# A three-block transformer kernel on one core: the opening's loads cut by partitions, and three late products and roots placed elsewhere

## The chip, the cores and the metric

The kernel runs on one core of a Trainium2 chip. The metric is the device time of the whole program in microseconds (us). The core has five engines that run side by side and meet only at semaphores: TensorE (PE in the rows, its weight load PEld), VectorE (DVE), ScalarE (ACT), GpSimd (POOL) and SyncE (SP). Transfers are issued here from the instruction streams of SP and ACT. Each of the two has a queue of its own (q1 for SP, q10 for ACT in the profile), and both queues are served by the core's 16 DMA engines.

## The reference, cut to what matters

Three transformer blocks work on one sequence of 512 tokens with 1024 channels, each a mixer and a SwiGLU feed-forward part with root-mean-square norms between them.

```python
def reference(x, ...):
    x = first_block(...)      # norm, x @ w_in, pooling + dilated attention, @ w_out, norm, swiglu
    return second_block(...)  # retention + swiglu, then stick-breaking attention + swiglu

def rms_norm(x, g):
    return x * lax.rsqrt(jnp.mean(x * x, axis=-1, keepdims=True) + EPS) * g

def stick_breaking(h, w_in, q_gain, k_gain, w_o):
    q, k, v = jnp.split(h @ w_in, 3, axis=-1)
    q = rms_norm_2(heads(q), q_gain)      # per head of 64
    k = rms_norm_2(heads(k), k_gain)
    ...
```

## The kernel before

**Layout.** Activations stand channels first: the input X is 8 chunks of 128 channels x 512 tokens, 256 KB each. A weight matrix is streamed as units, each giving 128 output channels: 8 chunks of 128x128 (512 KB), or 11 in the down projections.

**Three products for one.** To keep float32 accuracy at the faster matmul type, every operand is split in a high and a low part. ScalarE rounds a landed unit RAW to WH; GpSimd (VectorE in a few places) makes WL = RAW - WH. HH and HL are the high and low part of the input, MH and ML of the feed-forward's hidden values. A unit costs 24 matmuls in a bank B of PSUM: WH x HH and WH x HL for each chunk (`high_part`), then WL x HH for each chunk (`low_part`). The semaphores are `s_hi` and `s_lo` (a unit's WH, WL are ready), `s_hi_used` (WH may be overwritten), `s_unit` (the unit is complete), `s_h_hi` and `s_h` (HH, HL of a chunk are ready).

**The norm is applied late.** HH and HL are the unnormed input times its gain. Squares are added up in ACC, a matmul with the matrix MEAN (or MEANR) gives the mean over channels, ScalarE takes the root of it, and the result RB multiplies the outputs. So a mean can stand anywhere in TensorE's order between the sum being ready and the first use of the root.

**The order** of each engine is written by hand; there is no scheduler. Each engine runs its own list and waits at semaphores.

**The opening.** The first unit (`first_unit`) needs X and unit 0 of the weights, cut in halves of four chunks. SP issues the gains, X1, X2, the second half of unit 0, X4, X6, the first half of unit 1, then unit 2, the constants and so on. ACT issues X0, the first half of unit 0, X3, X5, X7 and the second half of unit 1, and then begins its own work: HH of chunks 0 and 1, WH of the first half of unit 0, HH 2 and 3, WH of the second half, HH 4 to 7, WH of unit 1, and the eight squares SQ4. VectorE makes HL of each chunk and both halves of WL0, then adds the squares. TensorE runs three warm-up products of zeros and then the first unit, chunk by chunk. GpSimd starts WL of unit 1 once all of HL is ready and WL of units 2 to 5 once all squares are added:

```python
pool.wait_ge(s_h, DC)
split_lo(Unit(1), chunks)
pool.wait_ge(s_sq_used, DC)
for n in range(2, 6):
    split_lo(Unit(n), chunks)
```

**Start of the first feed-forward part.** `first_units_after_post` runs three units at once, chunk by chunk, as the updated input arrives. Behind it come units u0+3 and u0+4 in `ffn`, with the mean of the new input (`mean_of_sum`) in the middle of u0+4's high part.

**First stage of the stick-breaking attention.** `stick_stage` projects q, k and v of a pair of heads. The means of squares per head (`head_mean`, 0 for q and 1 for k) stand in TensorE's order around the v unit u+2; ScalarE takes the roots (`rn`), VectorE makes QT and KT from them, and the score products L1184 wait for KT. In the first stage no earlier pair is worked on (`a is None`).

Of the kernel before, what the change touches and what calls it, by code (L numbers as in the profile page):

```python
# [128 lines left out]
def build(nc, ins, out_t):  # L129
    ctx = ExitStack()  # L130
    with ctx:
# [141 lines left out]
        s_second = sem("second_half_weights_landed")  # L273
# [73 lines left out]
        def high_part(pe, u, bank, chunks, xh, xl, k0=0, start=True, halfway=None):  # L347

            wh = WH[u.s]
            pe.wait_ge(s_hi, u.index + 1)  # L350
            for c in range(chunks):
                if halfway is not None and c == chunks // 2:
# [152 lines left out]
        def _(sp):  # L505
# [11 lines left out]
            for count, chunks, large in STRETCHES:  # L517
                stream = ins["w_large" if large else "w_small"].rearrange("u p (c n) -> u p c n", c=chunks)
                start = 0
                if first == 0:  # L520

                    sp.dma_start(GAINS[:], ins["gains"]).then_inc(s_gains, 16)
                    for c in (1, 2):
                        sp.dma_start(X[:, c, :], ins["x_t"][:, c, :]).then_inc(s_x_in[c], 16)
                    sp.dma_start(RAW[0][:, 4:DC, :], stream[0][:, 4:DC, :]).then_inc(s_raw[0], 16)
                    for c in (4, 6):
                        sp.dma_start(X[:, c, :], ins["x_t"][:, c, :]).then_inc(s_x_in[c], 16)
                    sp.dma_start(RAW[1][:, 0:4, :], stream[1][:, 0:4, :]).then_inc(s_raw[1], 16)
                    load_unit(Unit(2), stream[2], chunks)
                    sp.wait_ge(s_x_in[DC - 1], 16)  # L530
# [113 lines left out]
        def _(pe):  # L644
# [62 lines left out]
            def first_units_after_post(u0, which, n, mean):  # L707
# [27 lines left out]
                for bank, _, wl in units:  # L735
                    pe.matmul(bank[:], wl[:, DC - 1, :], HH[:, DC - 1, :], start=False, stop=True).then_inc(s_unit, 1)

            def ffn(f, u0, before, n=None):
# [10 lines left out]
                if before is None:  # L749
# [4 lines left out]
                    high_part(pe, Unit(u0 + 4), B[0][:], DC, HH, HL, halfway=lambda: mean_of_sum(n))  # L754
# [412 lines left out]
            def stick_stage(j, jp, a, ap):  # L1167
# [112 lines left out]
                else:  # L1280
# [43 lines left out]
        def _(act):  # L1324
# [133 lines left out]
            act.dma_start(X[:, 0, :], ins["x_t"][:, 0, :]).then_inc(s_x_in[0], 16)  # L1458
            act.preload_act_table_set(LOG_EXP)
            act.dma_start(RAW[0][:, 0:4, :], small[0][:, 0:4, :]).then_inc(s_first, 16)  # L1460
            for c in (3, 5, 7):
                act.dma_start(X[:, c, :], ins["x_t"][:, c, :]).then_inc(s_x_in[c], 16)
            act.dma_start(RAW[1][:, 4:DC, :], small[1][:, 4:DC, :]).then_inc(s_second, 16)
            act.wait_ge(s_gains, 16)
            for c in range(DC):
                act.wait_ge(s_x_in[c], 16)
                input_hi(c, G_MIX1)
                if c == 1:
                    act.wait_ge(s_first, 16)
                    act.copy(WH[0][:, 0:4, :], RAW[0][:, 0:4, :]).then_inc(s_first_hi, 1)  # L1470
                if c == 3:
                    act.wait_ge(s_raw[0], 16)
                    act.copy(WH[0][:, 4:DC, :], RAW[0][:, 4:DC, :]).then_inc(s_hi, 1)
            act.wait_ge(s_second, 16)
# [194 lines left out]
            def stick_stage(j, jp, a, ap):  # L1669
# [97 lines left out]
                if j is not None:  # L1767
# [52 lines left out]
        def _(dve):  # L1820
# [712 lines left out]
```

## Time and profile before

| | |
|---|---|
| three runs | 1969.74, 1970.10, 1970.29 us; median 1970.1 |
| profiled execution | 1969.64 us, of which span 1967.9 |
| TensorE busy | 1959.1 us of the span |
| VectorE, ScalarE, GpSimd busy | 860.4, 801.4, 769.4 us |
| moved by DMA | 177.37 MB, mean 90 GB/s |
| granted TensorE clock | 1.0 over the whole span |

The time of a run is the span plus what lies around it, 1.7 us in the profiled execution. TensorE's idle time is what is left over between 1967.9 and 1959.1, about 9 us over the whole kernel. The page's slices are 49 us wide, so places of a microsecond are read from the timeline instead.

### The profile page before, as it was taken

The page shows a single profiled execution, that of the slowest core. Times are in us where ns is not written, and L with a number is a line of the kernel's source. Part 1 is how long each engine was busy: PE and PEld are TensorE (multiplying, and loading weights), DVE is VectorE, ACT ScalarE, POOL GpSimd, SP SyncE. Part 2 cuts the span into 40 slices and gives each one's busy share as a digit, 9 for nine tenths or more (in the row PEclk, how much of TensorE's full clock was granted, in tenths as well). Part 3 has the DMA queues.
Part 4 walks back from the last instruction along what each step waited for, and adds up shares of the span by engine and source line. Part 5 has one row for each costly group of instructions (what it writes and reads, how often), then busy time and mean ns, then how long its engine had stood idle before and what let it go on. Part 6 is the DMA issues. An engine that isn't in the chain of part 4 may idle for free.

```text
span 1967.9 us, 25769 instructions
## 1 busy us (share of the span) xinstructions
PE 1959.1 (100%) x8956; PEld 1591.1 (81%) x8956; DVE 860.4 (44%) x1142; ACT 801.4 (41%) x1078; POOL 769.4 (39%) x309
## 2 busy tenths in 40 slices
PE   9999999999999999999999999999999999999999
PEld 6777888888888778787888888887777788888887
DVE  5775643433135335334243434224788753433200
ACT  6665533233243433324332223225888752323211
POOL 3223444444423334243444444433222144444443
PEclk9999999999999999999999999999999999999999
DMA  4212122223223222222232223222111122222332
GB/s 172 73 68 86 65 96 96 96 96 114 92 73 123 70 86 91 69 88 83 85 107 96 96 96 111 90 99 84 54 64 53 54 97 96 96 96 96 110 100 90
DMA packets 48867, 177.37 MB, mean 90 GB/s; under 512 B 5552, under 2 KB 6192, under 8 KB 48816
## 3 DMA queue, kind: packets, MB, share of 16 engines
q1 hardware_dynamic: 46656, 173.08, 26.1%
q10 hardware_dynamic: 2160, 3.61, 0.6%
q8 instruction: 33, 0.54, 0.1%
q14 instruction: 18, 0.15, 0.0%
HBM read 174.57 MB, written 2.10 MB: 90 GB/s over the span
## 4 chain that ended last, share of the span: by engine, by line
PE 96%; DVE 2%; ACT 1%; issue 0%; DMA 0%; POOL 0%; SPq 0%; DVEq 0%; ACTq 0%; POOLq 0%
PE B L354 26%; PE B L355 26%; PE B L363 25%; PE B L1068 2%; PE B L1195 1%; PE B L1026 1%; PE B L1030 1%; PE B L1027 1%; PE B L380 1%; PE B L375 1%; PE B L376 1%; PE B L1184 1%; PE B L1112 1%; PE B L1240 1%; PE B L854 1%; PE B L885 1%
## 5 line engine op out<-in xcount | busy, mean ns | idle before, releaser
L588 POOL TENSOR_TENSOR WL<-RAW,WH 128x1024 fp32r<-128x1024 f32 (+1 forms) x298 | 758.4, 2547 | 1173.1 <-PE B L363 768.9
L354 PE MATMUL B<-HH,WH 128*128 128x512 f32 x1608 | 629.2, 391 | 0.2 <-ACT WH L335 0.2
L355 PE MATMUL B<-HL,WH 128*128 128x512 f32 x1608 | 626.1, 389 | 0.0
L335 ACT CAST WH<-RAW 128x1024 fp32r<-128x1024 f32 (+1 forms) x300 | 329.1, 1098 | 550.9 <-PE B L355 478.7
L363 PE MATMUL B<-HH,WL 128*128 128x512 f32 x1608 | 398.3, 390 | 0.0
L354 PEld LDWEIGHTS B<-HH,WH 128*128 128x128 f32 x1608 | 301.9, 188 | 65.3 <-issue 2.3
L363 PEld LDWEIGHTS B<-HH,WL 128*128 128x128 f32 x1608 | 301.4, 188 | 63.1 <-POOL WL L588 0.4
L355 PEld LDWEIGHTS B<-HL,WH 128*128 128x128 f32 x1608 | 301.9, 188 | 62.4
L1850 DVE TENSOR_TENSOR U<-B,RB 128x512 f32<-128x512 f32 x66 | 45.6, 691 | 294.7 <-PE B L363 294.7
L354 PE MATMUL B<-MH,WH 128*128 128x512 f32 x440 | 171.2, 389 | 0.0
L355 PE MATMUL B<-ML,WH 128*128 128x512 f32 x440 | 171.2, 389 | 0.0
L1853 DVE TENSOR_TENSOR HD<-SG,U 128x512 f32<-128x512 f32 x66 | 148.5, 2251 | 7.4 <-ACT SG L1353 0.7
L1357 ACT CAST MH<-HD 128x512 f32 (+1 forms) x66 | 40.9, 620 | 247.3 <-DVE HD L1853 247.3
L1868 DVE TENSOR_TENSOR X<-X,B 128x512 f32 (+1 forms) x32 | 22.0, 687 | 244.2 <-PE B L363 223.2
L1833 DVE TENSOR_TENSOR ACC<-ACC,SQ 128x512 f32<-128x512 f32 x38 | 74.7, 1965 | 118.9 <-ACT SQ L1331 118.8
L363 PE MATMUL B<-MH,WL 128*128 128x512 f32 x440 | 106.2, 389 | 0.0
L354 PEld LDWEIGHTS B<-MH,WH 128*128 128x128 f32 x440 | 82.6, 188 | 17.1
L363 PEld LDWEIGHTS B<-MH,WL 128*128 128x128 f32 x440 | 82.6, 188 | 17.1
L355 PEld LDWEIGHTS B<-ML,WH 128*128 128x128 f32 x440 | 82.6, 188 | 17.1
L1353 ACT ACTIVATE SG<-G 128x512 f32<-128x512 f32 x66 | 41.8, 633 | 88.9 <-DVE G L1848 88.9
L1856 DVE TENSOR_TENSOR ML<-HD,MH 128x512 f32 (+1 forms) x66 | 49.4, 748 | 58.2 <-ACT MH L1357 58.2
L1848 DVE TENSOR_TENSOR G<-B,RB 128x512 f32<-128x512 f32 x66 | 45.6, 691 | 54.7 <-PE B L363 46.2
(349 smaller groups left out, 2246.9 us busy)
## 6 DMA issues: line engine op xcount, KB each, us to landing
RAW<-in_w_small SPq DMA_DIRECT2D x254, 512.0 KB, 3.2
RAW<-in_w_large SPq DMA_DIRECT2D x48, 704.0 KB, 4.1
out_t<-X SPq DMA_DIRECT2D x8, 256.0 KB, 5.1
X<-in_x_t ACTq DMA_DIRECT2D x4, 256.0 KB, 6.3
X<-in_x_t SPq DMA_DIRECT2D x4, 256.0 KB, 6.4
DECAY<-in_decay ACTq DMA_DIRECT2D x4, 256.0 KB, 2.7
RAW<-in_w_small ACTq DMA_DIRECT2D x2, 256.0 KB, 6.6
RAW<-in_w_small SPq DMA_DIRECT2D x2, 256.0 KB, 7.4
```

The lines of the kernel that those rows point to most:

```text
L335: act.copy(wh, raw).then_inc(s_hi, 1)
L354: pe.matmul(bank, wh[:, c, :], xh[:, k0 + c, :], start=(start and c == 0), stop=False)
L355: mm = pe.matmul(bank, wh[:, c, :], xl[:, k0 + c, :], start=False, stop=False)
L363: mm = pe.matmul(bank, wl[:, c, :], xh[:, k0 + c, :], start=False, stop=(stop and c == chunks - 1))
L588: pool.tensor_tensor(wl, raw, wh.bitcast(F32), ALU.subtract).then_inc(s_lo, 1)
L1353: act.activation(SG[:], G1[:], ACT.Silu).then_inc(s_silu, 1)
L1357: act.copy(MH[:, i, :], HD[:]).then_inc(s_m_hi, 1)
L1833: dve.tensor_tensor(ACC[:], ACC[:], SQ[b][:], ALU.add).then_inc(s_sq_used, 1)
L1848: dve.tensor_tensor(G1[:], gate, RB[:], ALU.mult).then_inc(s_gate, 1)
L1850: dve.tensor_tensor(U1[:], up, RB[:], ALU.mult).then_inc(s_up, 1)
L1853: dve.tensor_tensor(HD[:], SG[:], U1[:], ALU.mult).then_inc(s_hidden, 1)
L1856: dve.tensor_tensor(ML[:, i, :], HD[:], MH[:, i, :].bitcast(F32), ALU.subtract).then_inc(s_m, 1)
```

## The change

Four things are changed.

1. **Opening.** Each X chunk and both halves of unit 0 are loaded by two transfers: partitions 0 to 63 from ACT, partitions 64 to 127 from SP. Both queues have the same order: X0, X1, first half of unit 0, X2, X3, second half, X4 to X7, then unit 1 (its halves of four chunks over all 128 partitions, one on each queue as before). Whoever uses a chunk waits for 32 instead of 16. ACT issues X4 and X5 behind its HH 0, X6 and X7 behind HH 1, and its half of unit 1 behind HH 2.
2. **Three low products** of chunk 6 in `first_units_after_post` stand behind the high products of chunk 7, and the high products of chunk 6 wait for HL 6 at once.
3. **The mean** in unit u0+4 of the first feed-forward part stands behind five chunks instead of four.
4. **First stick-breaking stage:** the k mean stands behind six chunks of the v unit's high part instead of behind all eight, and ScalarE takes its root before it rounds unit u+3, not after.

```diff
-                    for c in (1, 2):
-                        sp.dma_start(X[:, c, :], ins["x_t"][:, c, :]).then_inc(s_x_in[c], 16)
-                    sp.dma_start(RAW[0][:, 4:DC, :], stream[0][:, 4:DC, :]).then_inc(s_raw[0], 16)
-                    for c in (4, 6):
-                        sp.dma_start(X[:, c, :], ins["x_t"][:, c, :]).then_inc(s_x_in[c], 16)
+                    for c in range(2):
+                        sp.dma_start(X[64:P, c, :], ins["x_t"][64:P, c, :]).then_inc(s_x_in[c], 16)
+                    sp.dma_start(RAW[0][64:P, 0:4, :], stream[0][64:P, 0:4, :]).then_inc(s_first, 16)
+                    for c in (2, 3):
+                        sp.dma_start(X[64:P, c, :], ins["x_t"][64:P, c, :]).then_inc(s_x_in[c], 16)
+                    sp.dma_start(RAW[0][64:P, 4:DC, :], stream[0][64:P, 4:DC, :]).then_inc(s_raw[0], 16)
+                    for c in range(4, DC):
+                        sp.dma_start(X[64:P, c, :], ins["x_t"][64:P, c, :]).then_inc(s_x_in[c], 16)
...
+            def load_x(c):
+                act.dma_start(X[0:64, c, :], ins["x_t"][0:64, c, :]).then_inc(s_x_in[c], 16)
...
             for c in range(DC):
-                act.wait_ge(s_x_in[c], 16)
+                act.wait_ge(s_x_in[c], 32)
                 input_hi(c, G_MIX1)
+
+                if c < 2:
+                    load_x(2 * c + 4)
+                    load_x(2 * c + 5)
+                if c == 2:
+                    act.dma_start(RAW[1][:, 4:DC, :], small[1][:, 4:DC, :]).then_inc(s_third, 16)
                 if c == 1:
-                    act.wait_ge(s_first, 16)
+                    act.wait_ge(s_first, 32)
                     act.copy(WH[0][:, 0:4, :], RAW[0][:, 0:4, :]).then_inc(s_first_hi, 1)
...
-                for c in range(DC - 1):
+                for c in range(DC - 2):
                     chunk(c, SECOND if c < BY_HALVES else slice(0, T), lambda: pe.wait_ge(s_h_hi, 8 * which + c + 1),
                           lambda: pe.wait_ge(s_h, 8 * which + c + 1))
+                pe.wait_ge(s_h, 8 * which + DC - 1)
+                for bank, wh, _ in units:
+                    pe.matmul(bank[:], wh[:, DC - 2, :], HH[:, DC - 2, :], start=False, stop=False)
+                    pe.matmul(bank[:], wh[:, DC - 2, :], HL[:, DC - 2, :], start=False, stop=False)
...
-                    high_part(pe, Unit(u0 + 4), B[0][:], DC, HH, HL, halfway=lambda: mean_of_sum(n))
+                    high_part(pe, Unit(u0 + 4), B[0][:], DC, HH, HL, halfway=lambda: mean_of_sum(n), at=5)
...
+                    else:
+                        high_part(pe, u + 2, B[0][:], DC, HH, HL, halfway=lambda: head_mean(1, 1), at=6)
...
+                        rn(1, jj, first)
                         split_hi(act, u + 3, DC)
-                        rn(1, jj, first)
                         split_hi(act, u + 4, DC)
```

**ScalarE at the start of the program**, before (its transfers and its work up to the four last chunks of the input):

```order
L1458 DMA X<-in_x_t 128x512
L1459 ACT_TABLE_LOAD
L1460 DMA RAW<-in_w_small 128x512
L1462 DMA X<-in_x_t 128x512 x3
L1463 DMA RAW<-in_w_small 128x512
L1334 ACTIVATE HH<-X,GAINS 128x512 x2
L1470 CAST WH<-RAW 128x512
L1334 ACTIVATE HH<-X,GAINS 128x512 x2
L1473 CAST WH<-RAW 128x512
L1334 ACTIVATE HH<-X,GAINS 128x512 x4
```

and now, up to HH of chunk 2:

```order
L1473 DMA X<-in_x_t 64x512
L1476 ACT_TABLE_LOAD
L1473 DMA X<-in_x_t 64x512
L1478 DMA RAW<-in_w_small 64x512
L1473 DMA X<-in_x_t 64x512 x2
L1481 DMA RAW<-in_w_small 64x512
L1347 ACTIVATE HH<-X,GAINS 128x512
L1473 DMA X<-in_x_t 64x512 x2
L1347 ACTIVATE HH<-X,GAINS 128x512
L1473 DMA X<-in_x_t 64x512 x2
L1494 CAST WH<-RAW 128x512
L1347 ACTIVATE HH<-X,GAINS 128x512
```

Before, all six of ScalarE's transfers (one above as L1458, one L1460, three L1462, one L1463) stood ahead of the first HH. Now six of half the partitions do, a pair stands behind HH 0 and a pair behind HH 1, both ahead of the first rounding of weights (`CAST WH<-RAW 128x512`); the whole one for unit 1 comes behind HH 2.

**TensorE at the end of `first_units_after_post`**, before (WH x HH, WH x HL and WL x HH of three units, the last two chunks):

```order
L717 MATMUL B<-HH,WH 128x512
L718 MATMUL B<-HH,WL 128x512
L723 MATMUL B<-HL,WH 128x512 x3
L733 MATMUL B<-HH,WH 128x512
L734 MATMUL B<-HL,WH 128x512
L733 MATMUL B<-HH,WH 128x512
L734 MATMUL B<-HL,WH 128x512
L733 MATMUL B<-HH,WH 128x512
L734 MATMUL B<-HL,WH 128x512
L736 MATMUL B<-HH,WL 128x512 x3
```

and now:

```order
L739 MATMUL B<-HH,WH 128x512
L740 MATMUL B<-HL,WH 128x512
L743 MATMUL B<-HH,WH 128x512
L744 MATMUL B<-HL,WH 128x512
L743 MATMUL B<-HH,WH 128x512
L744 MATMUL B<-HL,WH 128x512
L743 MATMUL B<-HH,WH 128x512
L744 MATMUL B<-HL,WH 128x512
L746 MATMUL B<-HH,WL 128x512
L747 MATMUL B<-HH,WL 128x512
L746 MATMUL B<-HH,WL 128x512
L747 MATMUL B<-HH,WL 128x512
```

L718 before was the WL x HH product of chunk 6, between its WH x HH (L717) and its WH x HL (L723). Now chunk 6's high products are L739 and L740, which alternate and so need its HL from the second on, and its three low products stand as L746 behind chunk 7's high ones (L743, L744), each ahead of chunk 7's low one (L747).

**ScalarE in the first stick-breaking stage**, before (root of the q mean, rounding of unit u+3, root of the k mean):

```order
L1800 ACTIVATE RQ<-B,GAINS 128x512
L1802 ACTIVATE RQ<-RQ 128x512
L335 CAST WH<-RAW 128x1024
L1800 ACTIVATE RQ<-B,GAINS 128x512
L1802 ACTIVATE RQ<-RQ 128x512
```

and now:

```order
L1825 ACTIVATE RQ<-B,GAINS 128x512
L1827 ACTIVATE RQ<-RQ 128x512
L1825 ACTIVATE RQ<-B,GAINS 128x512
L1827 ACTIVATE RQ<-RQ 128x512
L336 CAST WH<-RAW 128x1024 x2
```

The second root stands ahead of both roundings.

## Rows read from the trace of the kernel before

**Rows 1.** The page: busy time of each engine and share of the span.

```profile
PE 1959.1 (100%) x8956; PEld 1591.1 (81%) x8956; DVE 860.4 (44%) x1142; ACT 801.4 (41%) x1078; POOL 769.4 (39%) x309
```

**Rows 2.** Timeline of the opening (start us, length us, engine, line, operation, [idle before <-releaser]).

```profile
1.67 1.67 ACTq L1462 DMA_DIRECT2D X<-in_x_t  x3
...
4.35 0.72 ACT L1334 ACTIVATE HH<-X,GAINS 128x512 fp32r<-128x512 f32 x1 [1.87 <-DMA X<-in_x_t]
...
5.79 0.72 ACT L1334 ACTIVATE HH<-X,GAINS 128x512 fp32r<-128x512 f32 x1 [0.72 <-DMA X<-in_x_t]
...
6.42 0.60 ACT L1470 CAST WH<-RAW 128x512 fp32r<-128x512 f32 x1
...
7.89 1.41 DVE L1838 SCALAR_TENSOR_TENSOR HL<-X,GAINS,HH 128x512 fp32r<-128x512 f32 x2
...
9.37 0.69 DVE L1990 TENSOR_TENSOR WL<-RAW,WH 128x512 fp32r<-128x512 f32 x1
...
10.05 2.68 ACT L1334 ACTIVATE HH<-X,GAINS 128x512 fp32r<-128x512 f32 x4 [0.78 <-DMA X<-in_x_t]
...
10.88 2.76 DVE L1838 SCALAR_TENSOR_TENSOR HL<-X,GAINS,HH 128x512 fp32r<-128x512 f32 x4 [0.81 <-ACT HH L1334]
...
11.68 0.50 PE L950 MATMUL B<-HH,WH 128*128 128x512 f32 x1 [1.33 <-DVE HL L1838]
...
12.64 1.03 ACT L335 CAST WH<-RAW 128x1024 fp32r<-128x1024 f32 x1
...
14.78 0.39 PE L354 MATMUL B<-HH,WH 128*128 128x512 f32 x1
```

**Rows 3.** Single issue lines of the opening: start, and time from issue to landing.

```profile
L524 SPq DMA_DIRECT2D X<-in_x_t x2: 424/425/426, 1.2 to 1.7; - x2
...
DMA to landing us min/median/max: 4.6/5.0/5.4
...
L528 SPq DMA_DIRECT2D RAW<-in_w_small x1: 497/497/497, 3.8 to 3.8; - x1
...
DMA to landing us min/median/max: 8.3/8.3/8.3
```

**Rows 4.** Windows: PE, PEld, DVE, ACT, POOL busy; granted clock, DMA share, GB/s.

```profile
8.00:10.00 2.00, 1.83 (x9) 1.19 (x7) 1.92 (x3) 1.00 (x2) 0.00 (x0) 1.00 1.04 391
```

**Rows 5.** Timeline, units 1 and 2: VectorE, GpSimd, TensorE's weight load.

```profile
14.82 1.95 DVE L1893 TENSOR_TENSOR ACC<-SQ 128x512 f32<-128x512 f32 x1 [1.19 <-ACT SQ L1477]
...
21.64 4.73 POOL L588 TENSOR_TENSOR WL<-RAW,WH 128x1024 fp32r<-128x1024 f32 x2 [5.41 <-DVE ACC L1896]
...
24.29 0.19 PEld L363 LDWEIGHTS B<-HH,WL 128*128 128x128 f32 x1 [0.24 <-POOL WL L588]
```

**Rows 6.** Timeline, start of the first feed-forward part.

```profile
226.60 0.75 DVE L1915 SCALAR_TENSOR_TENSOR HL<-X,GAINS,HH 128x512 fp32r<-128x512 f32 x1
...
229.01 8.69 DVE L1896 TENSOR_TENSOR ACC<-ACC,SQ 128x512 f32<-128x512 f32 x6
...
231.40 0.69 DVE L1896 TENSOR_TENSOR ACC<-ACC,SQ 128x512 f32<-128x512 f32 x1
...
231.46 5.69 POOL L588 TENSOR_TENSOR WL<-RAW,WH 128x1024 fp32r<-128x1024 f32 x2 [20.66 <-ACT WH L335]
231.52 0.47 PE L354 MATMUL B<-HH,WH 128*128 128x512 f32 x1 [0.15 <-ACT WH L335]
...
239.22 0.47 PE L654 MATMUL B<-ACCH,MEANR 128*128 128x512 f32 x1 [0.20 <-DVE ACCL L1886]
```

**Rows 7.** Timeline, first stage of the stick-breaking attention.

```profile
1357.62 0.75 DVE L2346 SCALAR_TENSOR_TENSOR QT<-QS,GAINS,RQ 128x512 f32<-128x512 f32 x1 [0.56 <-ACT RQ L1802]
...
1358.20 0.39 PE L1259 MATMUL B<-SQH,HEADMEAN 128*128 128x512 f32 x1
...
1358.86 0.69 ACT L1800 ACTIVATE RQ<-B,GAINS 128x512 f32<-128x512 f32 x1 [0.33 <-PE B L1260]
...
1361.05 1.77 PE L1184 MATMUL B<-QT,KT 64*128 64x512 f32 x8 [0.42 <-DVE KT L2346]
```

More of the change, by code:

```diff
@@ L272, in build @@
         s_first = sem("first_half_weights_landed")
-        s_second = sem("second_half_weights_landed")
+        s_second = sem("rest_of_first_weights_landed")
+        s_third = sem("rest_of_second_weights_landed")
         s_first_hi = sem("first_half_weights_hi")
@@ L345, in use_unit, with high_part @@
             low_part(pe, u, bank, chunks, xh, k0, stop)
-        def high_part(pe, u, bank, chunks, xh, xl, k0=0, start=True, halfway=None):
+        def high_part(pe, u, bank, chunks, xh, xl, k0=0, start=True, halfway=None, at=DC // 2):
             wh = WH[u.s]
@@ L351, in high_part @@
             for c in range(chunks):
-                if halfway is not None and c == chunks // 2:
+                if halfway is not None and c == at:
                     halfway()
@@ L735, in first_units_after_post @@
                 for bank, _, wl in units:
+                    pe.matmul(bank[:], wl[:, DC - 2, :], HH[:, DC - 2, :], start=False, stop=False)
                     pe.matmul(bank[:], wl[:, DC - 1, :], HH[:, DC - 1, :], start=False, stop=True).then_inc(s_unit, 1)
@@ L1292, in stick_stage @@
                     pe.wait_ge(b_qs, jj * 2 + 1)
-                    high_part(pe, u + 2, B[0][:], DC, HH, HL, halfway=(lambda: head_mean(0, 7)) if a is not None else None)
                     if a is not None:
+                        high_part(pe, u + 2, B[0][:], DC, HH, HL, halfway=lambda: head_mean(0, 7))
                         later(0)
-                    head_mean(1, 1)
+                        head_mean(1, 1)
+                    else:
+                        high_part(pe, u + 2, B[0][:], DC, HH, HL, halfway=lambda: head_mean(1, 1), at=6)
                     low_part(pe, u + 2, B[0][:], DC, HH)
@@ L1457, in _ @@
             small = ins["w_small"].rearrange("u p (c n) -> u p c n", c=DC)
-            act.dma_start(X[:, 0, :], ins["x_t"][:, 0, :]).then_inc(s_x_in[0], 16)
+            def load_x(c):
+                act.dma_start(X[0:64, c, :], ins["x_t"][0:64, c, :]).then_inc(s_x_in[c], 16)
+            load_x(0)
             act.preload_act_table_set(LOG_EXP)
[L1460 to L1463, printed above, removed]
+            load_x(1)
+            act.dma_start(RAW[0][0:64, 0:4, :], small[0][0:64, 0:4, :]).then_inc(s_first, 16)
+            load_x(2)
+            load_x(3)
+            act.dma_start(RAW[0][0:64, 4:DC, :], small[0][0:64, 4:DC, :]).then_inc(s_second, 16)
             act.wait_ge(s_gains, 16)
             for c in range(DC):
-                act.wait_ge(s_x_in[c], 16)
+                act.wait_ge(s_x_in[c], 32)
                 input_hi(c, G_MIX1)
+                if c < 2:
[3 more added lines that the diff above has]
+                    act.dma_start(RAW[1][:, 4:DC, :], small[1][:, 4:DC, :]).then_inc(s_third, 16)
                 if c == 1:
-                    act.wait_ge(s_first, 16)
+                    act.wait_ge(s_first, 32)
                     act.copy(WH[0][:, 0:4, :], RAW[0][:, 0:4, :]).then_inc(s_first_hi, 1)
```

10 lines of the change are left out of this document (6 added, 4 removed).

## The prediction

> **What bounds the kernel now.** I read four views in this order. The page first: TensorE is busy 1959.1 us of a span of 1967.9 [rows 1], so all that any reordering can give back is the 8.8 us in which it stands still. VectorE, ScalarE and GpSimd are busy 39 to 44% [rows 1]; their work counts only where TensorE waits for it. The list of TensorE's waits then says where it stood, and the timeline at those places says for what. Every edit of this change lies at one of them.
>
> *The opening.* The reader is to see a chain, X landed, HH on ScalarE, HL on VectorE, product, of which the links are 0.72 and 0.75 us long while another can start every 0.67 to 0.69 us (four HH in 2.68, four HL in 2.76) [rows 2]. HH 0 starts at 4.35 after a wait for its transfer, HH 1 at 5.79 after another, the first rounding of weights at 6.42. HL 2 begins at 7.89. After HL 3 and the second WL0 (9.37, 0.69) VectorE stands still for 0.81 until 10.88, because HH 4 waited for X4 until 10.05; TensorE waits for HL 4 until 11.68, 1.33 of it idle [rows 2]. From there VectorE's four HL run without a pause to 13.64, and TensorE follows them chunk by chunk. So the end of the first unit is set by the end of HL 7, not by the first product.
>
> *The transfers.* X0 had landed by 4.3, when HH 0 starts [rows 2]. X1 landed at 5.8 (1.2 + 4.6), X2 at 7.1 (1.7 + 5.4), and the last of the twelve pieces of 256 KB at 12.1 (3.8 + 8.3) [rows 3]. Eleven pieces after the first in 7.8 us are 0.71 us a piece. Between 8 and 10 us all 16 engines are busy and move 391 GB/s [rows 4]: the opening's transfers are bound by bytes, and only their order is free.
>
> **Opening, new.** All pieces come in one order, each shared by both queues. The first lands a little later, since its upper half is behind the gains on SP's queue: I take 4.3. At 0.71 to 0.72 a piece the landings are X1 5.0, first half of unit 0 5.7, X2 6.5, X3 7.2, second half 7.9, X4 8.6, X5 9.3, X6 10.1, X7 10.8, unit 1 12.2. X4 comes 1.4 us earlier than its HH started before; the last piece comes no earlier.
>
> ScalarE now issues four transfers before its first rounding of weights. An issue is 0.42 us on SP [rows 3], and three in a row on ScalarE take 1.67, or 0.56 each [rows 2]. How long one of 64 partitions takes no row shows; the bounds are nothing and 0.56, and I take 0.5, between the two rows of whole ones, as if size did not enter. An issue overlaps the activation before it, as the transfers do with the table load, but the next activation waits for it. So: HH 0 at 4.4, HH 1 at 5.4 (two issues, X1 is there), rounding at 6.4 (two more). That is where it was, 6.42, and HL 2 again starts at about 7.9. The gain comes behind it: HH 2 to HH 7 find their chunks landed, and VectorE has seven pieces of work in a row (HL 2, HL 3, WL0, HL 4 to 7) at 0.69: 7.89 + 4.83 = 12.7, against 13.64. **Opening: -0.9 us.**
>
> Does it last? Three things must keep up. Rounding of unit 1 takes 1.03 and started at 12.64, behind HH 7 [rows 2]; now it starts when unit 1 lands, 12.2, and ends at 13.3, while TensorE asks for it 1.14 behind the end of HL 7 (14.78 against 13.64) [rows 2], so at about 13.9. Then WL of unit 2: GpSimd starts it when all squares are added, at 21.64, and TensorE's weight load for it was held until 24.29, 0.24 of it idle [rows 5]. Ahead of that load stands the float32 mean, which covers about 0.4. The sum's first addition took 1.95 where its like takes 0.69, blocked by GpSimd's WL of unit 1 [rows 5]; with that WL 0.5 earlier the whole row ends about 0.5 earlier, which with the cover gives TensorE its 0.9. If unit 1 lands 0.5 later than I take, half the gain is lost here. Last, the root that follows the mean moves with TensorE.
>
> **Low products of chunk 6.** Before, TensorE waited at the end: WH was freed by the second bank's last high product, ScalarE rounded unit u0+3, and the next unit began at 231.52 with 0.15 of idle time and a slow first product, 0.3 in all against a pace of 0.23 [rows 6]. Three products (0.68 us) now stand behind that release, so this wait is gone. But chunk 6's high products now need HL 6, which ends at 227.35 (226.60 + 0.75) [rows 6], when TensorE was done with chunk 5 at about 227.1: a new wait of 0.3. **Sum 0.** Bounds: -0.3 if HL 6 is in time, +0.1 if both stay.
>
> **The mean behind five chunks.** TensorE waited for ACCL until 239.22, idle 0.20, again with a slow restart, about 0.4 in all [rows 6]; a chunk more (0.45) in front covers it. What is late next: WH is freed 0.3 to 0.5 us sooner, so GpSimd's WL starts not at 231.46 but at about 231.1. VectorE's six additions took 8.69 where six alone take about 4.8, because the last two met GpSimd's two WL of 2.85 each [rows 6]. One of them began at 231.40, just ahead of GpSimd's 231.46 [rows 6]. With GpSimd ahead of it, it is blocked instead, and one more addition is left when GpSimd is done: ACC is ready 0.5 later. The cover of 0.45 is eaten. **Sum 0**, bounds -0.45 and +0.4.
>
> **Stick-breaking, first stage.** TensorE waited 0.42 for KT until 1361.05, nearly 0.6 with the slow restart. The chain: k mean at 1358.20, root from 1358.86, KT, score product, 2.19 us from root to product [rows 7]. The mean moves four products (0.9) up, but the root writes RQ, which QT still reads until 1357.62 + 0.75 = 1358.37 [rows 7]. So the root starts at 1358.4, not 1357.9, and KT is there for 1360.6, when TensorE arrives at 1360.5. **Sum -0.4.** Unit u+3's rounding goes behind both roots, to about 1360; its products start at 1364.4, so nothing waits.
>
> **Sum.** -0.9 + 0 + 0 - 0.4 = -1.3 us on the profiled execution's 1969.64: 1968.3. The median of the three runs lies 0.46 above that execution, so 1968.8. The rest of the kernel is bound by TensorE and keeps its length. A change within 0.2% (3.9 us) is about what a measurement of this kernel cannot tell from none.
>
> **Rivals.**
>
> *Halves move at half the rate (slower).* No row of this trace shows a transfer of fewer than 128 partitions. If an engine or a port could not serve both halves at once, ten pieces would come at 1.43 us instead of 0.72: X0 at 5.0, X7 at 17.8. HH 7 and HL 7 (0.72 and 0.75) follow 1.5 later, at 19.3 against 13.64, so +5.6, and unit 1 is as late. With -0.4 elsewhere: 1975.3, 0.26% slower. It costs more than it gives once a piece takes over 0.87 us (X7 after 12.1), and it is slower by 3.9 us from 1.34. For it: nothing in the trace. Against it: both queues are filled from 1 to 10 us and the 16 engines take from both [rows 4]. The Trainium skill, page "SBUF — State Buffer", section "Can I just issue two DMAs to hit both halves?", says no: two concurrent transfers, at partition 0 and at partition 64, gave only 6% over a single one. By that rule this rival is the forecast, and 1975 the time. I give it 11%, since it isn't clear that its two transfers came from two queues.
>
> *The gain is eaten.* Issues on ScalarE at 0.7 each (the longest of the five before), or pieces at 0.8 us because each now has its completion twice. The first puts the rounding at 7.2 and HL 7 at 13.6; the second puts unit 1 at 13.1 and its rounding at 14.2, late for TensorE. Opening 0 to -0.2, in all 1969.5 to 1970.3. 18%.
>
> *More gain.* Half issues at half the price: rounding at 5.8, HL 7 bound by X7 at 10.8 + 1.5 = 12.3, so -1.4; and if GpSimd does not overtake VectorE, -0.45 from the mean: 1967.8. 14%.
>
> *The change does nothing outside the opening* (KT late all the same): 1969.2, inside the forecast's own spread.
>
> **Chances.** Forecast, with its spread 1968.3 to 1969.4: 55%. Eaten 18%, more gain 14%, half rate 11%, and 2% for a gain over 3.9 us, which would need nearly half of all of TensorE's idle time back. The range 1967.5 to 1971.2 leaves out the half rate and little more. Faster by over 0.2%: 2%; within: 87%; slower: 11%.
>
> **What the profile after would show.** Right: HH 0 near 4.4, rounding near 6.4, no wait for X4, HL 7 done near 12.7, the first product of unit 1 near 13.9 instead of 14.78. At the feed-forward start a wait for HL 6 in place of that for WH, and still one for ACCL. KT's wait shorter than 0.2. Wrong: a DMA rate near 200 GB/s between 4 and 10 us, or HH 1 after 5.8. What would make the prediction wrong is above all the rate of the halves, then the landing of unit 1.

## The result: 1973.9 us, slower by 0.21%

The changed kernel takes 1973.92 us (median of 18 runs, 1972.71 to 1976.22), the kernel before 1969.86 (18 runs, 1969.31 to 1970.29). The ratio is 1.0021, with an interval of 1.0015 to 1.0027: 4.06 us slower, just over the 3.9 us (0.2%) that the prediction took as no difference. The forecast of 1968.8 was wrong, and so was its range, which ended at 1971.2. The changed kernel also scatters more, over 3.5 us instead of 1.0.

The profiled execution took 1973.12 us with a span of 1971.3; before it was 1969.64 and 1967.9. The page again shows TensorE with the same instructions (against [rows 1]):

```profile
PE 1959.9 (99%) x8956; PEld 1592.1 (81%) x8956; DVE 864.0 (44%) x1142; ACT 801.6 (41%) x1078; POOL 769.4 (39%) x309
```

Its busy time grew by 0.8 us only; the other 2.6 us by which the span grew are new idle time. To find where, I compared the start of the same product in both traces. The table shows how much later it starts than before.

| Place | later by, us |
|---|---|
| first product of unit 0 (7.92 against 7.08) | 0.84 |
| first product of unit 1 (16.35 against 14.78) | 1.57 |
| 25.6 us, in unit 2 | 1.58 |
| 36 us, in unit 4 | 4.20 |
| 231.5 us, first product of unit u0+3 at the start of the first feed-forward part | 4.31 |
| 241 us, behind the mean in the feed-forward part | 3.76 |
| 1362 us, score products of the stick-breaking attention | 3.37 |
| end of the span | 3.45 |

So two losses lie in the first 36 us, 1.6 and 2.6; 0.11 us is lost at the edited low products, and two gains of 0.55 and 0.39 come behind them.

**First loss: the opening.** Timeline of the changed kernel (columns as in [rows 2]):

```profile
4.73 0.72 ACT L1347 ACTIVATE HH<-X,GAINS 128x512 fp32r<-128x512 f32 x1 [2.10 <-DMA X<-in_x_t]
4.75 1.16 ACTq L1473 DMA_DIRECT2D X<-in_x_t  x2
...
5.96 0.72 ACT L1347 ACTIVATE HH<-X,GAINS 128x512 fp32r<-128x512 f32 x1 [0.51 <-DMA X<-in_x_t]
...
7.25 0.62 ACT L1494 CAST WH<-RAW 128x512 fp32r<-128x512 f32 x1 [0.57 <-issue]
...
7.92 0.50 PE L961 MATMUL B<-HH,WH 128*128 128x512 f32 x1 [1.98 <-ACT WH L1494]
...
10.04 0.62 ACT L1498 CAST WH<-RAW 128x512 fp32r<-128x512 f32 x1 [0.85 <-DMA RAW<-in_w_small]
...
12.60 0.73 ACT L1347 ACTIVATE HH<-X,GAINS 128x512 fp32r<-128x512 f32 x1 [0.32 <-DMA X<-in_x_t]
...
13.69 0.72 ACT L1347 ACTIVATE HH<-X,GAINS 128x512 fp32r<-128x512 f32 x1 [0.36 <-DMA X<-in_x_t]
...
14.51 0.75 DVE L1863 SCALAR_TENSOR_TENSOR HL<-X,GAINS,HH 128x512 fp32r<-128x512 f32 x1 [0.33 <-ACT HH L1347]
...
14.73 1.05 ACT L336 CAST WH<-RAW 128x1024 fp32r<-128x1024 f32 x1 [0.32 <-DMA RAW<-in_w_small]
...
16.35 0.39 PE L355 MATMUL B<-HH,WH 128*128 128x512 f32 x1
```

The reader is to see the releasers. Before, only HH 4 waited for its chunk in the second half of the opening, and four HL ran in a row to 13.64 [rows 2]. Now HH 6 and HH 7 wait for their chunks (12.60, 13.69), HL 7 ends at 15.26, and the rounding of unit 1 waits for its own transfer until 14.73. The transfers are late, and this is how late, with what an issue of 64 partitions takes (issue lines as in [rows 3], SP's halves of X4 to X7 and of unit 1):

```profile
L532 SPq DMA_DIRECT2D X<-in_x_t x4: 596/597/597, 5.0 to 6.9; - x4
...
DMA to landing us min/median/max: 5.9/6.1/6.8
...
L533 SPq DMA_DIRECT2D RAW<-in_w_small x1: 585/585/585, 7.5 to 7.5; - x1
...
DMA to landing us min/median/max: 7.1/7.1/7.1
```

X7 landed at 13.7 (6.9 + 6.8), the last piece at 14.6 (7.5 + 7.1). From 4.7, when HH 0 starts, that is nine more pieces in 9.0 us and eleven in 9.9: 1.0 and 0.90 us a piece, where I had taken 0.71 to 0.72. The windows show the same as a rate (columns as in [rows 4]):

```profile
4.00:6.00 2.00, 1.95 (x4) 0.55 (x2) 0.40 (x1) 0.76 (x2) 0.00 (x0) 1.00 1.01 276
6.00:8.00 2.00, 0.08 (x1) 0.08 (x1) 1.13 (x3) 1.43 (x3) 0.00 (x0) 1.00 0.86 271
8.00:10.00 2.00, 2.00 (x6) 1.57 (x7) 2.00 (x3) 1.19 (x2) 0.00 (x0) 0.59 0.87 269
10.00:12.00 2.00, 2.00 (x7) 1.47 (x5) 0.96 (x3) 1.67 (x3) 0.00 (x0) 0.56 1.04 300
```

And of the kernel before, ahead of the line in [rows 4]:

```profile
4.00:6.00 2.00, 2.00 (x4) 0.67 (x2) 0.75 (x1) 0.93 (x2) 0.00 (x0) 1.00 0.99 352
6.00:8.00 2.00, 1.73 (x5) 0.67 (x4) 1.38 (x3) 1.98 (x4) 0.00 (x0) 1.00 0.99 356
```

It is 269 to 300 GB/s now, where it was 352 to 391, although the DMA engines are busy 0.86 to 1.04 of the time. It is neither the full rate nor the "near 200" of the rival. The last but one column shows a second thing: TensorE stood idle for 1.98 us ahead of 7.92, and from 8.4 to 11.8 us its granted clock is 0.5, the 1.2 GHz level; before it was 1.00 in that window.

**Second loss: units 2 to 4.** Timeline of the kernel before, GpSimd and VectorE where the rotary tables CS and SN are scaled:

```profile
26.30 0.69 DVE L1999 TENSOR_TENSOR CS<-CS,RB 128x512 f32<-128x512 f32 x1 [4.74 <-ACT RB L1345]
26.91 0.69 DVE L1999 TENSOR_TENSOR SN<-SN,RB 128x512 f32<-128x512 f32 x1
27.28 2.58 POOL L588 TENSOR_TENSOR WL<-RAW,WH 128x1024 fp32r<-128x1024 f32 x1 [0.91 <-ACT WH L335]
```

And of the changed kernel:

```profile
23.75 4.75 POOL L593 TENSOR_TENSOR WL<-RAW,WH 128x1024 fp32r<-128x1024 f32 x2 [5.40 <-DVE ACC L1921]
...
27.87 1.18 DVE L2025 TENSOR_TENSOR CS<-CS,RB 128x512 f32<-128x512 f32 x1 [4.20 <-ACT RB L1358]
...
28.86 2.44 POOL L593 TENSOR_TENSOR WL<-RAW,WH 128x1024 fp32r<-128x1024 f32 x1 [0.36 <-ACT WH L336]
28.97 2.88 DVE L2025 TENSOR_TENSOR SN<-SN,RB 128x512 f32<-128x512 f32 x1
...
31.88 0.69 DVE L2068 TENSOR_TENSOR RT<-B,CS 128x512 f32<-128x512 f32 x1
...
36.50 0.50 PE L355 MATMUL B<-HH,WH 128*128 128x512 f32 x1 [2.77 <-DVE QT L2076]
```

GpSimd's two WL ended at 26.37 before (21.64 + 4.73, [rows 5]), just as CS began. Now they end at 28.50, 2.1 later, since GpSimd starts them when all squares are added, and ScalarE takes the squares behind the rounding of unit 1, which came late. VectorE, released by TensorE's mean and the root, is only 1.6 later (27.87 against 26.30). So CS meets the second WL and takes 1.18. SN then starts at 28.97, just behind GpSimd's WL of unit 4 (28.86), and takes 2.88 instead of 0.69. Everything behind it on VectorE is late, and TensorE waits 2.77 us for QT, where before the same product came at 32.25.

The later edits are seen in the last group (timeline of the changed kernel, feed-forward start and stick-breaking):

```profile
231.57 0.19 PEld L739 LDWEIGHTS B<-HH,WH 128*128 128x128 f32 x1 [0.51 <-DVE HL L1940]
...
234.26 2.00 ACT L336 CAST WH<-RAW 128x1024 fp32r<-128x1024 f32 x2 [2.13 <-PE B L744]
...
235.68 5.63 POOL L593 TENSOR_TENSOR WL<-RAW,WH 128x1024 fp32r<-128x1024 f32 x2 [20.73 <-PE B L747]
...
243.53 0.39 PE L659 MATMUL B<-ACCH,MEANR 128*128 128x512 f32 x1
...
1364.42 1.77 PE L1195 MATMUL B<-QT,KT 64*128 64x512 f32 x8
```

The wait for ACCL is gone (0.20 at 239.22, [rows 6]), and so is TensorE's 0.42 for KT [rows 7].

### The profile page after: what moved, and what is told of

It reads as the page before. It is cut to its first block, busy times and chain, and to the rows that moved or that the text cites. A ratio compares the mean times of both kernels' runs of the same rounds, so it can differ in the third digit from the quotient of the medians.

```text
span 1971.3 us, 25780 instructions
## 1 busy us (share of the span) xinstructions
PE 1959.9 (99%) x8956; PEld 1592.1 (81%) x8956; DVE 864.0 (44%) x1142; ACT 801.6 (41%) x1078; POOL 769.4 (39%) x309
## 4 chain that ended last, share of the span: by engine, by line
PE 97%; DVE 1%; ACT 1%; issue 0%; DMA 0%; SPq 0%; POOL 0%; ACTq 0%; DVEq 0%; POOLq 0%
PE B L355 26%; PE B L356 26%; PE B L364 25%; PE B L1079 2%; PE B L1206 1%; PE B L1037 1%; PE B L1041 1%; PE B L1038 1%; PE B L381 1%; PE B L377 1%; PE B L376 1%; PE B L1195 1%; PE B L1123 1%; PE B L1251 1%; PE B L865 1%; PE B L896 1%
```

## Experiments

My theory after the result: the opening carries the whole loss, in two parts, late transfers because they span 64 partitions, and the collision of SN with GpSimd that their lateness sets off. The rivals: the three later edits cost something (my own term of +0.4 for the mean); the transfers are late because there are twice as many, or because of where ScalarE issues them; the clock at 0.5 explains it.

Differences below are between medians, each kernel against the kernel before on the same chip: 1969.87 (29 runs) for experiments 1 to 4, 1969.71 (33 runs) for 5, 6, 7 and 9, and 1969.67 (27 runs) for 8, 10 and 11.

### 1. The opening alone

The changed kernel, with the feed-forward and stick-breaking edits undone (cut; the k mean also goes back behind all eight chunks):

```diff
-                for c in range(DC - 2):
+                for c in range(DC - 1):
...
-halfway=lambda: mean_of_sum(n), at=5)
+halfway=lambda: mean_of_sum(n))
...
-                        rn(1, jj, first)
                         split_hi(act, u + 3, DC)
+                        rn(1, jj, first)
```

> The changed opening alone; the three later places as in the kernel before. If the opening carries the whole loss and the later places give back 0.4 to 0.9 us, as the two traces place them (a shift of +4.3 us at 231 us, +3.4 at the end), this takes 4.5 to 5.0 us more than the kernel before: about 1974.6. If the loss came from a later place (the rival), it is at or below the changed kernel's 1973.9.

Measured: 1975.19 (7 runs, 1974.19 to 1976.34), ratio 1.0027 (1.0016 to 1.0039), +5.3 us. TensorE's list of waits has 2.8 us for QT and 1.8 for the first weights, as in the changed kernel, and 0.4 for KT. The opening alone loses more than the whole change. The profiled execution (1976.30) shows one thing more: behind the wait for QT TensorE's clock is at the 1.2 GHz level again, and from 37.8 to 40.4 us its products come 0.43 us apart instead of 0.23. A window:

```profile
38.00:40.00 2.00, 2.00 (x7) 1.52 (x6) 1.17 (x2) 1.92 (x4) 1.42 (x1) 0.50 0.00 0
```

The profile of the changed kernel has the same wait, and there the clock stays at 1.00 behind it.

### 2. The three later edits alone

The kernel before, with the same edits made, and the old opening (its edit, cut):

```diff
-                for c in range(DC - 1):
+                for c in range(DC - 2):
...
-halfway=lambda: mean_of_sum(n))
+halfway=lambda: mean_of_sum(n), at=5)
...
+                        rn(1, jj, first)
                         split_hi(act, u + 3, DC)
-                        rn(1, jj, first)
```

> The opening of the kernel before with the three later edits. Theory of the opening: 0.8 to 0.9 us faster than the kernel before, 1969.0 (the mean behind five chunks -0.5, the stick-breaking stage -0.4, the low products 0 to +0.1). Rival, the later edits cost something that the opening's shift hid: 1969.9 or more.

Measured: 1968.93 (11 runs, 1968.73 to 1969.29), ratio 0.9996 (0.9986 to 1.0005), -0.94 us. In its trace 0.5 is gained by 241 us, behind the mean, and 0.45 by 1362. The edits gain, and nothing of the loss is theirs. With experiment 1 the sum is 5.32 - 0.94 = 4.38, against 4.06 for the whole.

### 3. Halves by columns instead of by partitions

The same number of transfers in the same places, of half the tokens or chunks of all 128 partitions:

```diff
-sp.dma_start(X[64:P, c, :], ins["x_t"][64:P, c, :])
+sp.dma_start(X[:, c, T // 2:T], ins["x_t"][:, c, T // 2:T])
...
-sp.dma_start(RAW[0][64:P, 4:DC, :], stream[0][64:P, 4:DC, :])
+sp.dma_start(RAW[0][:, 6:DC, :], stream[0][:, 6:DC, :])
```

> The changed kernel, but each piece of the opening is cut by columns (tokens 0-255 and 256-511 of a chunk; two weight chunks and two) and both transfers cover all 128 partitions; queues, order, counts and waits are the same. If the cut at 64 partitions is what slows issue (0.56 to 0.69 us) and movement (about 275 GB/s), issues fall back to 0.42 to 0.45 us, movement to over 340 GB/s, HL 7 ends near 13, and the time is about 1969 to 1970. Rival, that twice as many transfers cost it whatever their shape: issues and landings stay as in the changed kernel, 1973 to 1974; descriptors of 1 KB for X could even make it slower.

Measured: 1970.67 (11 runs, 1969.11 to 1971.51), ratio 1.0004 (0.9995 to 1.0013), +0.8. Windows:

```profile
6.00:8.00 2.00, 0.00 (x0) 0.00 (x0) 0.46 (x2) 0.95 (x2) 0.00 (x0) 1.00 0.97 321
8.00:10.00 2.00, 1.55 (x4) 1.28 (x5) 1.97 (x4) 2.00 (x4) 0.00 (x0) 0.52 1.10 381
```

From 8 to 10 us twice as many transfers move 381 GB/s when they span all partitions, against 269 in the changed kernel. So from 8 us on the number of transfers alone does not cost the rate; before that it is 264 and 321, against 352 and 356 in the kernel before. But the opening gains next to nothing by it: X1 comes late, HH 1 starts at 6.89, HH 6 waits for its chunk until 12.88, HL 7 ends at 15.11 and not near 13, and unit 1's first product is late by 1.46 all the same. The collision is absent here (CS 27.79 and SN 28.40, each 0.69), which by experiment 4 is most of the 3.3 us that it is faster. The rows of X are half as long in memory, so this doesn't test the partitions by themselves; experiment 5 is the better one.

### 4. The collision taken away

The changed kernel, in which GpSimd's WL of unit 4 waits until CS and SN are scaled:

```diff
                     for n in range(2, 6):
+                        if n == 4:
+                            pool.wait_ge(s_dve, 2)
                         split_lo(Unit(n), chunks)
```

> The changed kernel with one wait added: GpSimd makes WL of unit 4 only after VectorE has scaled the cosine and sine tables. If the second half of the loss (from +1.6 us at 25.6 to +4.2 at 36 us) is VectorE blocked by that WL, SN takes 0.69 instead of 2.88 us, TensorE's wait of 2.8 us for QT falls to about 0.6, and the time to about 1971.7. Rival, the loss is simply the late opening carried along: no change, 1973.9.

Measured: 1971.18 (11 runs, 1970.77 to 1971.70), ratio 1.0007 (0.9998 to 1.0016), +1.31. That is 2.75 less than the changed kernel's +4.06, and the scatter falls from 3.5 to 0.9 us. Timeline:

```profile
27.97 1.30 DVE L2027 TENSOR_TENSOR CS<-CS,RB 128x512 f32<-128x512 f32 x1 [4.08 <-ACT RB L1360]
...
29.19 0.68 DVE L2027 TENSOR_TENSOR SN<-SN,RB 128x512 f32<-128x512 f32 x1
...
29.95 2.40 POOL L593 TENSOR_TENSOR WL<-RAW,WH 128x1024 fp32r<-128x1024 f32 x1 [1.23 <-DVE SN L2027]
...
34.52 0.50 PE L355 MATMUL B<-HH,WH 128*128 128x512 f32 x1 [0.55 <-DVE QT L2078]
```

SN is back at 0.68 and TensorE's wait for QT falls from 2.77 to 0.55. The collision of SN with WL of unit 4 is worth 2.75 us, shown by this one wait.

Two things are left open by it. CS still takes 1.30, since it meets the second of the two WL ahead (24.0 to 28.7), which the added wait doesn't move; it costs about 0.5 us, as TensorE is late by 1.80 at the start of unit 3 (28.36) and by 2.27 behind QT. And some of the 2.75 may be the clock. In the changed kernel's 18 runs the three with a mean granted clock of 1.000 took 1972.78 to 1972.94 us, and the two with 0.997, the lowest, were the slowest, 1975.64 and 1976.22. A second stretch at the lower level behind a wait of 2.8 us, as in experiment 1's profile, would fit; no trace of such an execution of the changed kernel was taken, so this isn't shown.

### 5. Every second partition instead of an upper and a lower half

Experiment 4, with the same 64 partitions a transfer, but taken from the whole width:

```diff
-X[64:P, c, :], ins["x_t"][64:P, c, :]
+X[1:P:2, c, :], ins["x_t"][1:P:2, c, :]
...
-X[0:64, c, :], ins["x_t"][0:64, c, :]
+X[0:P:2, c, :], ins["x_t"][0:P:2, c, :]
```

> As e_port_order (1971.2), but the 64 partitions of a transfer are every second one: even ones from ACT, odd ones from SP. Sizes, counts, rows of 2 KB and waits are the same. If the low rate (250 to 300 GB/s) comes from a transfer reaching only one half of the partitions, the rate goes over 340 and the time to 1970.3 or less. Rival, that 64 partitions, or twice as many transfers, cost it wherever they lie: 1971.2, rate under 300.

Measured: 1969.85 (11 runs, 1969.58 to 1970.94), ratio 1.0001 (0.9992 to 1.0010), +0.14: 1.17 less than experiment 4. The issues cost the same, 0.60 us on SP. A window and the timeline of the opening:

```profile
10.00:12.00 2.00, 2.00 (x5) 1.62 (x6) 1.83 (x4) 1.93 (x4) 0.00 (x0) 0.51 1.05 403
```

```profile
10.49 2.64 ACT L1349 ACTIVATE HH<-X,GAINS 128x512 fp32r<-128x512 f32 x4
...
11.32 2.74 DVE L1865 SCALAR_TENSOR_TENSOR HL<-X,GAINS,HH 128x512 fp32r<-128x512 f32 x4
```

With the same count of transfers, bytes and partitions, four HH again run without a wait, and HL 7 ends at 14.06. The rate is 403 GB/s from 10 to 12 us, against 265 in experiment 4's own trace and 300 in the changed kernel's; before 8 us it is 261 and no better, which I hadn't expected. So which 64 partitions a transfer covers is worth 1.2 us, but the traces show it only from 8 us on. The edit changes the rows of memory that a transfer reads along with the partitions that it fills, and no run tells the two apart.

Against experiment 2 there is still a loss of 1.1 us (0.14 + 0.94), and this trace parts it in two: unit 1's first product is late by 0.52 against the kernel before (15.30), as is that of unit 3 (27.08), and the product behind QT by 0.98 (33.23), because CS meets GpSimd's second WL here as well and takes 1.16.

### 6. ScalarE's issues ahead of HH 0

Experiment 4, with ScalarE's halves of X4 to X7 and of unit 1 issued ahead of the first activation:

```diff
+            for c in range(4, DC):
+                load_x(c)
+            act.dma_start(RAW[1][:, 4:DC, :], small[1][:, 4:DC, :]).then_inc(s_third, 16)
...
-                if c < 2:
-                    load_x(2 * c + 4)
-                    load_x(2 * c + 5)
```

> As e_port_order, but ScalarE issues X4 to X7 and its half of unit 1 ahead of its first HH. If issues between its activations hold the first rounding (7.25 against 6.42) and through it the first product, but not the end of HL 7 (which waits for X7), the time stays at 1971.2 within 0.4: HH 0 moves from 4.7 to about 7.3 and eats what it saves. If the issues' position is what costs the opening, it falls to 1970.3 or lower.

Measured: 1971.42 (11 runs, 1970.99 to 1972.14), ratio 1.0009 (1.0000 to 1.0018), +1.71, or 0.4 over experiment 4. Timeline:

```profile
7.96 1.33 ACT L1349 ACTIVATE HH<-X,GAINS 128x512 fp32r<-128x512 f32 x2 [5.33 <-issue]
...
12.69 2.73 DVE L1863 SCALAR_TENSOR_TENSOR HL<-X,GAINS,HH 128x512 fp32r<-128x512 f32 x4
```

HH 0 starts 3.2 us later than in experiment 4, and HL 7 ends at 15.42 against 15.37 there. X7 is taken up at 13.67 against 13.79, so its landing hardly moved, and the rate from 4 to 12 us is again 268 to 294 GB/s. So the late start of the chain is made up behind it, and the issues' position is not what makes the transfers slow; moving them ahead gains nothing.

### 7. A fourth warm-up of TensorE

Experiment 4, with four rounds of warm-up products instead of three:

```diff
-            for n in range(3):
+            for n in range(4):
```

> As e_port_order with four warm-up products instead of three, so TensorE's pause before its first product shrinks from 2.0 to about 0.3 us. If the granted clock falls to half after that pause and the opening's chunks are slowed by it, the clock stays 1.0 between 8 and 12 us; the end of the first unit is set by HL 7, so the median falls by 0.2 to 0.5 (1970.8) and the spread of 0.9 shrinks to that of the kernel before's (0.7). Rival: the clock is no cause, 1971.2.

Measured: 1970.69 (11 runs, 1970.37 to 1971.58), ratio 1.0006 (0.9997 to 1.0015), +0.98, 0.3 less than experiment 4. Window:

```profile
10.00:12.00 2.00, 1.53 (x6) 0.77 (x5) 1.87 (x4) 1.82 (x3) 0.00 (x0) 1.00 1.07 299
```

The granted clock stays at 1.00 (2.4 GHz) where it was 0.56 in experiment 4's profile. But the landings came earlier too in this profiled execution: HL 7 ends at 14.56, against 15.37 in experiment 4's. And the two kernels' runs overlap. So the low level of the opening is worth 0.3 us at most here and isn't the cause of the loss; nor is it that of experiment 4's scatter, 1.2 us here against 0.9. The changed kernel's own scatter of 3.5 was not tested in this way.

### 8. The fourth warm-up with every second partition

Experiments 5 and 7 together:

```diff
-X[64:P, c, :], ins["x_t"][64:P, c, :]
+X[1:P:2, c, :], ins["x_t"][1:P:2, c, :]
...
-            for n in range(3):
+            for n in range(4):
```

> e_every_second (1969.85) with four warm-up products. The clock stays at full rate from 8 to 12 us. If the slow clock costs as in e_warm4_port (0.5), 1969.4; if the end of HL 7 alone sets the first unit, 1969.8.

Measured: 1969.87 (11 runs, 1969.33 to 1970.07), ratio 1.0000 (0.9991 to 1.0010), +0.20, against +0.14 in experiment 5. The clock is at 1.00 from 6 to 12 us, and it gives nothing, since TensorE follows HL 4 to 7 chunk by chunk and these do not move (HL 7 ends at 14.05). A window:

```profile
8.00:10.00 2.00, 1.29 (x5) 0.86 (x5) 1.65 (x3) 1.97 (x4) 0.00 (x0) 1.00 1.01 379
```

With experiment 7 this is a second pair for the partitions, with the clock at full rate in both: +0.98 with halves, +0.20 with every second partition, 0.78 apart, and each against its own kernel before no run of the one reaches into those of the other. The rates of the pairs from 8 to 10 and from 10 to 12 us: halves 269 and 300 GB/s (changed kernel), 280 and 265 (experiment 4), 268 and 288 (6), 329 and 299 (7); every second partition 298 and 403 (5), 379 and 355 (8).

### 9. Without the edit on low products

Experiment 2, without moving chunk 6's low products:

```diff
-                for c in range(DC - 2):
+                for c in range(DC - 1):
```

> As e_late_only (1968.93) without the edit of the three low products. The trace of the changed kernel loses 0.1 us at the place of that edit. If it costs that, this is 1968.8; if what it does for the release of WH pays later, it is 1969.0 or more.

Measured: 1968.89 (11 runs, 1968.65 to 1969.41), ratio 0.9996 (0.9987 to 1.0005), -0.82 against experiment 2's -0.94. The low products are worth nothing that can be told; the gain is the two means'.

### 10 and 11. Whole transfers, in a better order

Experiment 2 with GpSimd's wait of experiment 4 is the control (10):

```diff
+                        if n == 4:
+                            pool.wait_ge(s_dve, 2)
                         split_lo(Unit(n), chunks)
```

In 11 X4 goes to ScalarE's queue and X5 to SP's, each transfer whole, so that each chunk is taken up in its turn:

```diff
-                    for c in (4, 6):
+                    for c in (5, 7):
...
-            for c in (3, 5, 7):
+            for c in (3, 4, 6):
```

> e_late_only with only that added wait of GpSimd, the control for e_late_swap: the two did not meet in the kernel before (tables scaled from 26.30, GpSimd done at 26.37), so no change is expected, 1968.9. If the near miss costs in some runs, up to 0.3 less and a narrower spread.

> As e_late_only (whole transfers), but X4 and X6 go out on ScalarE's queue and X5 and X7 on SP's, so that chunks land in the order of their use; GpSimd's WL of unit 4 waits for the scaled tables, as in e_port_order. If the 1.4 us that HL 4 waits for X4 can be won by order alone, HL 4 starts near 10.0 instead of 10.9, HL 7 ends near 12.9, and the time is 0.6 to 0.8 below e_late_only: 1968.2. If the last pieces set the end instead (X7 now lands at about 11.4), 1968.9.

Measured: the control 1968.93 (11 runs, 1968.32 to 1969.19), ratio 0.9996 (0.9987 to 1.0005), -0.74; the new order 1968.37 (11 runs, 1967.93 to 1969.01), ratio 0.9994 (0.9985 to 1.0003), -1.30, the fastest kernel here. Timeline of the control, then of the new order:

```profile
10.35 2.68 ACT L1343 ACTIVATE HH<-X,GAINS 128x512 fp32r<-128x512 f32 x4 [0.74 <-DMA X<-in_x_t]
11.18 2.76 DVE L1847 SCALAR_TENSOR_TENSOR HL<-X,GAINS,HH 128x512 fp32r<-128x512 f32 x4 [0.65 <-ACT HH L1343]
```

```profile
9.46 2.88 ACT L1343 ACTIVATE HH<-X,GAINS 128x512 fp32r<-128x512 f32 x4
...
10.35 2.84 DVE L1847 SCALAR_TENSOR_TENSOR HL<-X,GAINS,HH 128x512 fp32r<-128x512 f32 x4
```

The control's HL 4 waits for X4's HH; in the new order it doesn't, and HL 7 ends at 13.19 against 13.94. Unit 1's first product comes 0.80 earlier (14.30 against 15.10), and in the medians 0.56 us of it is left. The rest goes where CS meets GpSimd's second WL once more; timeline of the new order:

```profile
25.84 0.93 DVE L2008 TENSOR_TENSOR CS<-CS,RB 128x512 f32<-128x512 f32 x1 [4.60 <-ACT RB L1354]
```

The product behind QT is 0.56 earlier. The wait on GpSimd costs nothing where there is no collision. The intervals of the ratios take in 1. What speaks for a gain is that every run of 10 and 11 (highest 1969.19 and 1969.01) lies under the median of the kernel before, 1969.67, and that ten of the eleven runs of the new order lie under 1968.70, the control's second lowest.

## Why the prediction was wrong

**The rate of the halves: the step that failed.** I wrote "At 0.71 to 0.72 a piece the landings are [...] X7 10.8, unit 1 12.2", since both queues were full before and all engines busy. It was 1.0 to X7 and 0.90 to unit 1; they landed at 13.7 and 14.6. [Rows 4] showed that the engines take from both queues, not that a transfer with half the partitions goes as fast. Experiment 5 wins 1.2 us by spreading the same 64 partitions, and experiments 7 and 8 are 0.8 apart by the same edit, so which 64 a transfer covers (with the rows of memory that it reads) is a cause, shown. It is part of the 2.25 us that experiment 4 leaves to the opening (1.31 + 0.94). The other 1.1 are there with spread partitions too: about 0.5 is CS meeting GpSimd's second WL, read from the trace of experiment 5, and about 0.5 is an opening that is late all the same. For that I have only the rates from 4 to 8 us, 222 to 321 GB/s in the traces with twice as many transfers (the changed kernel, experiments 1 and 3 to 8) and 298 to 380 in those with whole ones (the kernel before, experiments 2, 9, 10 and 11); that their number or their issues do it is argued, not shown.

The rival named this mechanism and set the point at 0.87 us a piece, "it costs more than it gives"; 0.90 to 1.0 lies behind it. But I gave it 11% and only the full price of half the rate. That its 1975.3 lies near the 1973.9 measured is luck: it has 5.6 us for the transfers, where all of the opening but the collision of SN cost 2.3, and it doesn't have that collision. Of the Trainium skill, page "SBUF — State Buffer", section "Can I just issue two DMAs to hit both halves?", the trace bears out the direction: two transfers, one on each half, don't add up to one over all partitions. Its size is not borne out: 6% over the rival's 1.43 us a piece would be 1.35, and 0.90 to 1.0 was measured. I set the rule aside because its two transfers might have come from one queue; no row stood behind that, and that section of the Trainium skill says itself that issuing from several engines doesn't help.

**The price of an issue.** I took 0.5; it is 0.60 (0.52 to 0.69), over both of the whole ones, 0.42 and 0.56 [rows 2, 3], for half the bytes. The rounding started at 7.25, not 6.4, near the 7.2 of the rival with issues at 0.7 each. Experiment 6 shows that this alone costs little: with HH 0 three us later HL 7 ends 0.05 later, and the time is 0.4 longer. The landings were the bound, as the rival "gain is eaten" had it in its second half, at a piece of 0.8.

**"Does it last? Three things must keep up."** I followed unit 1's landing to the rounding and to WL of unit 2, and wrote "if unit 1 lands 0.5 later than I take, half the gain is lost here". It landed 2.4 later. And the last sentence, "the root that follows the mean moves with TensorE", was true (CS 1.6 later), but I did not lay it beside GpSimd, which hangs on the landing and moved by 2.1. The two had missed each other by nothing: WL ended at 26.37, CS began at 26.30. That gap stood in the trace before. The collision, 2.75 us, is more than half of the opening's +5.3 (experiments 4 and 1). So this is the second step that failed: a term that the sum has at nothing, and the larger one. I had used the very mechanism at two other places, the sum's first addition and the feed-forward's additions.

**Low products: 0, right.** The wait for HL 6 came (the weight load stood idle for 0.51 until 231.57, and the shift of the products grew by 0.25 there), the one for WH went; in the trace 0.1 us of loss is left of both, and experiment 9 puts the edit at 0.1 or less.

**The mean behind five chunks: sum 0, measured -0.5.** The cover was right, what is late next was not. I had GpSimd start 0.4 earlier with WH. WH was rounded earlier, by 0.38 (234.26 less the shift of 4.31 is 229.95, against 230.33), but GpSimd's row names another releaser, TensorE's low products (L747), which the change had moved ahead of it. It started within 0.1 of before and blocked the same additions, six in 8.68. So the end of the range I had as a bound, -0.45, was the value.

**Stick-breaking: -0.4, measured -0.39 to -0.45**, by the steps given. TensorE no longer waits for KT.

**The sum.** -0.94 for the later edits against my -0.4; for the opening +5.3, or some 5.0 within the whole change, against my -0.9. Had only the rate been wrong, with no collision, the kernel would stand at about 1971.2 (experiment 4), the upper end of my range and 2.4 above my forecast.

## What to carry to other kernels

To have a row of transfers arrive in order, give each queue whole transfers over all 128 partitions and choose the order; splitting each into an upper and a lower half cost 0.8 to 1.2 us more here than splitting by every second partition, and even that was 1.1 us slower than whole ones. Where a delay of 1 to 2 us is put in, list the pairs of VectorE and GpSimd work behind it that only just miss each other: one such pair turned 1.6 us into 4.2, and one wait on GpSimd took 2.75 back. A chain that comes earlier can run into such a pair as well: 0.24 of 0.80 us was lost so in experiment 11. A new transfer shape whose rate no row shows should get a range as wide as the rival that stands for it.

## What the runs showed of the hardware

Transfers of 64 partitions, lower halves from one queue and upper halves from the other, moved 269 to 300 GB/s between 4 and 12 us in the changed kernel (244 to 329 with experiments 1, 4, 6 and 7), with the DMA engines shown busy 0.86 to 1.04. Whole transfers moved 352 to 391 in the kernel before, and 366 to 400 from 8 to 10 us in the five traces that have them. Every second partition moved 222 to 288 up to 8 us and 298 to 403 from 8 to 12 (experiments 5 and 8).

To issue a transfer of 64 partitions of X took 0.60 us in the median, lower or upper half or every second one alike. Of all 128 with half the tokens it took 0.43 (ScalarE's eight) and 0.54 (SP's last four). The twelve whole ones took 0.41 to 0.71, 0.45 in the median. Half the partitions isn't half the price. An activation waits for the issues ahead of it on its engine: behind five more of them HH 0 started at 7.96 in experiment 6, against 4.72 in experiment 4.

A VectorE operation with both inputs in SBUF took 2.88 us instead of 0.69 when GpSimd had started a WL of 2.44 us 0.1 ahead of it. The Trainium skill, page "SBUF — State Buffer", section "Who interferes with whom", has such an operation contend with a GpSimd one that reads SBUF; the trace agrees with its 2.88 us.

After 1.98 us without work TensorE's clock fell to the 1.2 GHz level from 8.4 to 11.8 us, and products came 0.43 us apart instead of 0.23. Without that fall the kernel was 0.3 us faster (experiment 7, runs overlapping) or no faster (experiment 8). The same wait doesn't always bring a fall: behind 2.78 us for QT the clock was at 0.50 in experiment 1's profile, and behind 2.77 us at 1.00 in the changed kernel's.
